# Four experts on three tiles of 128 rows, in column groups, and a gather that skips empty places

## What is computed

```python
def hierarchical_moe(x, ...):
    lg = (xt @ w_router_group + b_router_group)
    gsel = argmax(lg); pgsel = softmax(lg)[gsel]
    le_sel = (xt @ w_router_expert[gsel] + b_router_expert[gsel])
    vals, eidx = lax.top_k(le_sel, 2)
    pw = softmax(vals) * pgsel
    out = sum over the two experts e of pw[e] * (silu(x @ gate[e]) * (x @ up[e])) @ down[e]
y = layer_norm(alpha * h + out)
```

## Time and profile before

| | us |
|---|---|
| median of three runs | 1551.05 (1545.45 to 1553.15) |
| profiled execution, its own time | 1560.32 |
| its span | 1558.7 |
| PE busy in the span | 1439.7 (92%), 5,707 matmul and as many weight load records |
| DVE busy | 724.5 (46%) |
| bytes moved | 221.89 MB |
| granted PE clock, mean | 0.966 |

### The profile page before, as it was taken

The page is one execution under the profiler, slowest core; times in us unless marked ns, Lnnn a source line. Parts: engine busy times, 40 slices in busy tenths (PEclk is TensorE's granted clock), DMA queues, the critical chain, the costliest instruction groups (busy, mean ns, idle before and its releaser), DMA issues. The chain is left out here.

```text
span 1558.7 us, 17701 instructions
## 1 busy us (share of the span) xinstructions
PE 1439.7 (92%) x5707; PEld 782.1 (50%) x5707; DVE 724.5 (46%) x1639; ACT 297.2 (19%) x656; POOL 254.4 (16%) x308
## 2 busy tenths in 40 slices
PE   7999999799999999898989898999489999999985
PEld 2444444344566666565757564555244444444431
DVE  0201023788888889954648444566411111111125
ACT  0100122221221111102554200000011111111114
POOL 3131000133310000201351000011112111121103
PEclk9999999799999999998999899999689999999998
DMA  9221001400122111101331196111089999989835
GB/s 312 69 65 35 15 15 69 129 0 1 41 95 75 70 61 61 70 19 51 92 92 62 55 345 260 28 37 32 15 334 337 347 342 345 352 337 354 325 125 227
DMA packets 72474, 221.89 MB, mean 142 GB/s; under 512 B 16634, under 2 KB 42234, under 8 KB 62042
## 3 DMA queue, kind: packets, MB, share of 16 engines
q1 hardware_dynamic: 56138, 184.64, 33.0%
q0 software_dynamic: 14992, 35.90, 6.6%
q10 hardware_dynamic: 1280, 0.53, 0.2%
HBM read 190.56 MB, written 38.84 MB: 147 GB/s over the span
## 5 line engine op out<-in xcount | busy, mean ns | idle before, releaser
L1786 PE MATMUL main_ps_experts<-w_gate_up,main_e_rowsT 128*128 128x512 f32 x512 | 227.7, 598 | 1.2 <-DVE main_e_rowsT L1891 1.2
L906 DVE TENSOR_SCALAR_CACHE_REDUCE front<-score,bound 128x384 bf16<-128x384 f32 (+2 forms) x198 | 174.2, 943 | 19.2 <-DVE bound L932 18.9
L234 PE MATMUL ps_front<-front,x_all 128*128 128x512 f32 (+1 forms) x448 | 180.4, 557 | 1.7 <-ACT wi L364 1.7
L1786 PEld LDWEIGHTS main_ps_experts<-w_gate_up,main_e_rowsT 128*128 128x128 f32 x512 | 95.7, 192 | 110.6 <-issue 110.6
L234 PEld LDWEIGHTS ps_front<-front,x_all 128*128 128x128 f32 x448 | 83.2, 190 | 91.7 <-issue 81.2
L1896 DVE TENSOR_TENSOR main_hidden<-main_hidden,main_ps_experts 128x256 f32<-128x256 f32 x32 | 13.5, 421 | 221.1 <-ACT main_hidden L1843 221.1
L1520 PE MATMUL ps_merge<-w_o,mergedT 128*128 128x512 f32 x256 | 113.4, 601 | 3.0 <-DVE h_rows L1651 3.0
L733 PE MATMUL ps_gate<-x_all,w_gate 128*128 128x344 f32 x384 | 116.0, 461 | 0.0
L1813 PE MATMUL main_ps_experts<-w_down,main_hiddenT 128*128 128x512 f32 x256 | 115.3, 593 | 0.5 <-ACT main_hiddenT L1848 0.5
L733 PE MATMUL ps_gate<-x_all,front 128*128 128x344 f32 x384 | 113.2, 453 | 0.0
L733 PEld LDWEIGHTS ps_gate<-x_all,w_gate 128*128 128x128 f32 x384 | 74.3, 194 | 38.9 <-issue 2.4
(11 more groups left out here) (296 smaller groups left out, 1784.0 us busy)
## 6 DMA issues: line engine op xcount, KB each, us to landing
w_gate_up<-in_w_gate_up SPq DMA_DIRECT2D x32, 2048.0 KB, 8.7
w_down<-in_w_down SPq DMA_DIRECT2D x32, 1024.0 KB, 11.9
w_gate_up<-pair_out SPq DMA_DIRECT2D x8, 1024.0 KB, 12.0
front<-in_w_qkvi SPq DMA_DIRECT2D x8, 930.0 KB, 20.0
w_gate<-in_w_gate SPq DMA_DIRECT2D x4, 1280.0 KB, 6.0
front<-in_w_gate SPq DMA_DIRECT2D x4, 1280.0 KB, 5.9
h_rows<-in_x_rows SPq DMA_DIRECT2D x9, 512.0 KB, 6.0
h<-h_rows SPq DMA_DIRECT2D x18, 256.0 KB
```

Of the source, the lines that this page charges most:

```text
L234: mm = nc.tensor.matmul(ps[:, g % 2, 0:c1 - c0], x_all[:, k, t * P:(t + 1) * P], w[:, k, c0:c1], start=(k == 0), stop=(k == KC - 1))
L906: V.tensor_scalar(waste[0:n, at - width:at], s, column(bound, g), None, compare, ALU.add, accum_out=column(number, g)).then_inc(taken, 1)
L1786: mm = nc.tensor.matmul(ps[:, GU, :], rowsT[j][:, k, :], w_gu[jw][:, k, :], start=(k == 0), stop=(k == KC - 1))
```

## The change

Lists are cut into shares of 96 ranks. The shares of four experts fill three tiles of 128 rows ("packs"), 24 in all where there were 32 tiles: expert 0 takes rows 0 to 95 of the first, expert 1 its rows 96 to 127 and rows 0 to 63 of the second, expert 2 the other half of that and rows 0 to 31 of the third, expert 3 the rest. A list longer than 96 would bring a second pass. The matmuls of a pack go by column groups, four of 32 or two of 64, each with its own expert's weights as the moving operand. Gate/up and down weights get semaphores of their own, and a buffer is refilled as soon as its own last reader is through. The loop is unrolled. `place` works out lane, tile and share. The gather gets a bound, so that places past a list's end are skipped; the first two gathers still fetch 128 rows (their numbers are clamped), so that the buffers hold finite numbers.

```diff
+SHARE = 96
+QUAD = 4
+PACKS = N_EXPERTS // QUAD * 3
+PARTS = (((0, 32, 0), (32, 64, 0), (64, 96, 0), (96, 128, 1)), ((0, 64, 1), (64, 128, 2)),
+         ((0, 32, 2), (32, 64, 3), (64, 96, 3), (96, 128, 3)))
...
-                step(V.scalar_tensor_tensor(marked, ps[:, 3 + i % 2, 0:N_EXPERTS], float(N_EXPERTS), expert[:],
-                                            ALU.mult, ALU.add))
+                ranks = ps[:, 3 + i % 2, 0:N_EXPERTS]
+                step(V.tensor_scalar(share, ranks, 683.0, None, ALU.mult))
+                step(V.tensor_scalar(share, share, 16, None, ALU.logical_shift_right))
...
+                step(V.scalar_tensor_tensor(marked, wrap, 1.0 - P * PACKS, address, ALU.mult, ALU.add))
                 for which in range(2):
-                    step(V.tensor_tensor(waste, choice[which][i % 2][:], marked, ALU.mult))
-                    step(V.tensor_reduce(slot[:, which:which + 1], waste, AX.X, ALU.add))
+                    step(V.scalar_tensor_tensor(waste, choice[which][i % 2], 1.0, marked, ALU.mult, ALU.mult,
+                                                accum_out=slot[:, which:which + 1]))
...
-                if j >= 2:
-
-                    sp.wait_ge(rows_in[j - 2], 16)
-                load(j, j)
+            for e in range(loaded, W_BUFS):
+                load_gate_up(e)
+                load_down(e)
...
-                    sp.wait_ge(down, (i * W_BUFS + (j - W_BUFS)) * 2 + 2)
-                    load(i * W_BUFS + j, j)
+            for g in range(1, N_EXPERTS // QUAD):
+                e, s = g * QUAD, 3 * (g - 1)
+                sp.wait_ge(gate_up, s + 1)
+                load_gate_up(e)
+                sp.wait_ge(gate_up, s + 2)
+                load_gate_up(e + 1)
+                sp.wait_ge(down, 2 * s + 2)
+                load_down(e)
+                sp.wait_ge(gate_up, s + 3)
+                load_gate_up(e + 2)
+                load_gate_up(e + 3)
+                sp.wait_ge(down, 2 * s + 4)
+                load_down(e + 1)
+                sp.wait_ge(down, 2 * s + 6)
+                load_down(e + 2)
+                load_down(e + 3)
...
-                                            in_offset=bass.IndirectOffsetOnAxis(ap=tokens[:, e:e + 1], axis=0)
-                                            ).then_inc(rows_in[e % 2], 16)
+                                            in_offset=bass.IndirectOffsetOnAxis(ap=tokens[:, e:e + 1], axis=0),
+                                            bounds_check=TOK - 1, oob_is_err=False).then_inc(rows_in[e % 2], 16)
...
-                    mm = nc.tensor.matmul(ps[:, GU, :], rowsT[j][:, k, :], w_gu[jw][:, k, :], start=(k == 0), stop=(k == KC - 1))
+                    for c0, c1, b in PARTS[s % 3]:
+                        mm = nc.tensor.matmul(ps[c0:c1, GU, :], rowsT[j][:, k, c0:c1], w_gu[b][:, k, :],
+                                              start=(k == 0), stop=(k == KC - 1))
...
-            staggered(pe, N_EXPERTS, [(2, turn_hidden), (1, make_hidden), (0, turn_rows), (2, make_result)], W_BUFS)
+            staggered(pe, PACKS, [(2, turn_hidden), (1, make_hidden), (0, turn_rows), (2, make_result)], 2, loop=False)
...
-        with nc.If(longest > P):
+        with nc.If(longest > SHARE):
```

More of the change, by code:

```diff
@@ L1380, in merge_and_route @@
         empty = h[:, TILES - 1, 0:SLOTS // P].bitcast(U32)
-        fall, expert = sb("fall", [P, N_EXPERTS]), sb("expert", [P, N_EXPERTS])
+        fall, lane, column = (sb(n, [P, N_EXPERTS]) for n in ("fall", "lane", "column"))
         valid, away = sb("valid", [P, TILES]), sb("away", [P, TILES])
@@ L1389, in merge_and_route @@
         lgT = over[0:ROUTER, D + 3 * N_EXPERTS:D + 3 * N_EXPERTS + P]
-        choice = [[sb(f"choice{n}_{j}", [P, N_EXPERTS]) for j in range(2)] for n in range(2)]
-        both = [sb(f"both{j}", [P, N_EXPERTS]) for j in range(2)]
+        FREE = D + 3 * N_EXPERTS + P
+        free = [over[:, FREE + n * N_EXPERTS:FREE + (n + 1) * N_EXPERTS] for n in range(10)]
+        choice = [free[2 * n:2 * n + 2] for n in range(2)]
+        both = free[4:6]
+        share, lin, address, wrap = free[6].bitcast(I32), free[7], free[8], free[9]
         slot = sb("slot", [P, 2])
@@ L1688, in sem @@
             return nc.alloc_semaphore(f"{tag}_{name}")
-        ident, tokens, entries, w_gu, w_dn = (keep[n] for n in ("ident", "tokens", "entries", "w_gate_up", "w_down"))
-        w_in = keep["w_in"] if loaded else [sem(f"w_in{j}") for j in range(W_BUFS)]
+        ident, w_gu, w_dn = (keep[n] for n in ("ident", "w_gate_up", "w_down"))
+        tokens, entries = (keep[n][:, 0:PACKS] for n in ("tokens", "entries"))
+        w_gu_in, w_dn_in = (keep[n] if loaded else [sem(f"{n}{j}") for j in range(W_BUFS)] for n in ("w_gu_in", "w_dn_in"))
         rows = [sb(f"e_rows{j}", [P, D]) for j in range(2)]
@@ L1723, in _, with load_gate_up, load_down @@
         def _(sp):
[L1724 to L1730, removed]
-                if j >= 2:
-                    sp.wait_ge(rows_in[j - 2], 16)
-                load(j, j)
+            def load_gate_up(e):
+                sp.dma_start(w_gu[e % W_BUFS][:], ins["w_gate_up"][e]).then_inc(w_gu_in[e % W_BUFS], 16)
+            def load_down(e):
+                sp.dma_start(w_dn[e % W_BUFS][:], ins["w_down"][e]).then_inc(w_dn_in[e % W_BUFS], 16)
+            lists = scratch["list_of"].rearrange("(c p n) o -> c p (n o)", p=P, n=PACKS)
+            sp.dma_start(entries, lists[bass.ds(chunk, 1)]).then_inc(list_in, 16)
+            for e in range(loaded, W_BUFS):
+                load_gate_up(e)
+                load_down(e)
             if loaded:
@@ L1740, in _ @@
                                  ).then_inc(keep["f_const_in"], 16)
[L1741 to L1745 removed]
+            for g in range(1, N_EXPERTS // QUAD):
[14 more added lines that the diff above has]
+                load_down(e + 3)
             if loaded:
[L1747 removed]
+                sp.wait_ge(down, 2 * PACKS)
                 for j in range(2):
[L1749 removed]
+                    sp.wait_ge(stored[j], 16 * PACKS // 2)
                 last.sync(sp)
@@ L1754, in _ @@
             pool.wait_ge(tokens_ready, 1)
-            for e in range(N_EXPERTS + 3):
-                if e < N_EXPERTS:
+            for e in range(PACKS + 3):
+                if e < PACKS:
                     if e >= 2:
@@ L1903, in read_down @@
                 nc.vector.tensor_copy(result[j][:, 512:D], ps[:, 5 + 2 * j, :]).then_inc(down_dve, 1)
[L1905 removed]
+            staggered(dve, PACKS, [(1, multiply), (0, read_rows), (2, read_down)], 2, loop=False)
             if loaded:
@@ L2162, in build @@
         keep["w_down"] = [sb(f"w_down{j}", [P, F // P, D], side="right") for j in range(W_AHEAD)]
-        keep["w_in"] = [whole.enter_context(nc.semaphore(f"w_in_expert{j}")) for j in range(W_BUFS)]
+        keep["w_gu_in"], keep["w_dn_in"] = ([whole.enter_context(nc.semaphore(f"{n}_expert{j}")) for j in range(W_BUFS)]
+                                            for n in ("w_gu_in", "w_dn_in"))
         for name, shape, dt in (("router_logits", [P, TILES, ROUTER], F32), ("weights", [P, 2, TILES], F32),
```

64 lines of the change are left out of this document (38 added, 26 removed).

## The result

The change takes 1476.14 us (median of 4 runs, 1475.54 to 1480.27); the kernel before, on the same chip, 1550.64. The ratio is 0.9543, 95% interval 0.9511 to 0.9574, or 71 us of 1551. The profiled execution took 1475.57, with a span of 1474.1.

What follows compares the result with a forecast made beforehand. PE was taken to bound the experts stage before, the loads after. Last result at 1433.3 + 3.7 for routing = 1437.0 instead of 1503.8, 66.8 us less: 1551.05 - 66.8 = 1484 us, range 1466 to 1520.

Steps and rivals of the forecast that it cites:

- PE's own end: Experts stage: last result at 1420.0 us if PE alone set the pace, with 23 packs of 11.35 after the first product.
- A pack costs what an expert cost, 11.35: Experts stage: column groups overlap, so a pack takes 11.35 us and 24 stand where 32 stood.
- So I charge nothing: PE in the experts stage: turning between full width and column groups was taken to cost nothing, 0.13 us at most.
- The loads set the pace at 395 GB/s: Experts stage: transfers at 395 GB/s put the last result at 1433.3 us, later than PE's 1420.0.
- The later start: Start of the experts stage: first gather lands later among weight loads, first product ends at about 1151.2 us, +6.
- Routing +3.7: Routing: `place` has 12 DVE instructions instead of 6, lengthening routing by 3.7 us (between 2 and 5).
- Finish is the same: Finish, behind the experts stage: its 55 us hardly touched by the change.
- the lower rate: Rival, experts stage: full queues don't hold 395 GB/s; 1510 us at 359, 1526 at 340; chance 0.14.
- the fallen clock: Rival, experts stage: PE's clock falls in its waits, five waits losing 3 us each, 1499 us; chance 0.04.
- fetched rows: Rival, gathers: skipped rows are fetched all the same, 3.9 MB more, 10 us, 1494 us; chance 0.04.
- instruction supply: Rival, unrolled experts stage: PE waits for its instruction blocks, up to 1644 us; chance 0.05.
- Groups in series: Rival, packed matmuls: column groups don't overlap in a long row, +492 us, 2040 us; chance 0.03.

Runs made afterwards that it cites:

- e9: The kernel before with only the gathers' skip of places past a list's end, still 32 tiles; ratio 1.0005 to the kernel before.
- e3: The change with full-width matmuls and half of each weight block loaded from expert 4 on; stage 292.2 us, ratio 0.9452 to the kernel before.
- e11: The change with steps grouped by width, groups of 32, POOL's scatter a step later, first weight loads behind two gathers; stage 299.0 us, ratio 0.9502.
- e1: The change with full-width matmuls using one expert's weights instead of column groups, all loads kept; stage 298.1 us, ratio 0.9511 to the kernel before.
- e12: The change with the first tile of each three in groups of 96 and 32 columns; stage 410.4 us, ratio 1.0192 to the kernel before.
- e7: The change with PE, ACT and DVE steps put together by width and all groups of 32; stage 343.6 us, 1511.1 us.

## Why the prediction was right

The time was forecast at 1484, it was 1476.1, and the range held it. The sum was 66.8 us less; the ratio gives 71. The largest step, a quarter of PE's work in the stage, carried the direction and most of the size. That the number came so close is luck: PE's own end was forecast 11.6 us too early (1420.0 for 1431.6) and the loads' 15.4 too late (1433.3 for 1417.9), as worked out below, and the wrong one of the two was taken as the bound.

- *What bounds before*: PE's products. e9 takes 7.9 MB of transfers away from it and the time stays.
- *A pack costs what an expert cost, 11.35*: the matmuls do (7.07 against 7.03, 3.65 against 3.60), the pack doesn't. **"So I charge nothing" is the step that failed.** Four changes of width cost 0.15 us each, 0.6 a pack and 14 over the stage. e3, without changes and without the loads' limit, takes 13.6 less, and packs with two changes last 11.68. (The Trainium skill, "TensorEngine Tiling (Array Packing)", Key Properties, says that a change of mode drains the array; I held against it. The runs agree with the page: the weight loads no longer run ahead across a change.) The earlier trace rows held the loss, but I misread them. The merged rows show one shape; kept apart, a quarter of the full-width records move only 324 columns and not 512 (17 to 43 us: line, shapes, count | us busy, mean ns of one | idle before):

```profile
L219 PE MATMUL ps_front<-front,x_all 128*128 128x512 f32 x36 | 18.0, 610 | 0.0
L219 PE MATMUL ps_front<-front,x_all 128*128 128x324 f32 x12 | 4.2, 436 | 0.0
```

At 6.87 / 16 = 0.43 us for a record of 512 and 0.27 for one of 324, six and two of them and the small set's two would take 3.98 us, and the period is 4.31. By this estimate a change there and back costs some 0.33, about twice 0.15, and not the 0.13 at most that I took.
- *The loads set the pace at 395 GB/s*: they didn't. They ran at 410 and could do 418 to 420. By the prediction's own formula, 420 for 395 puts the end of the last result at 1417.9 in its time scale (1126.2 + 1.5 + 9 + 102.4 / 0.420 + 37.4), while PE's own end, with packs of 11.98, lies at 1125.8 + 305.8 = 1431.6 on the same scale. What I forecast as the loads' 307.5 us from request to end was PE's 305.8. (The Trainium skill, "DMA: Bandwidth & Descriptors", Specifications, has some 358 GB/s of HBM per core; 410 over 205 us on this one core are more.)
- *The later start*: the first product was to end 25.4 us after the request (1151.2 - 1125.8); it ended 24.7 after it (1140.05 - 1115.36).
- *Routing +3.7*: +3.6 between the same marks, but that it is so close is luck too. The same routing code took 240.2 (e11) to 244.7 us (e1) in other executions, and the old one 238.6 in e9. `place` itself grew from 1.28 to 2.39, so by 1.1 and not 1.6 us; the rest I didn't take apart.
- *Finish is the same*: it was 54.9 and 55.0 us with the old routing and lists (before, e9) and 52.0 to 53.4 in all other runs. Why it is 2 us shorter is open.
- *Rivals*: the lower rate, the fallen clock (1.00 from 1150 to 1400 us), fetched rows and instruction supply didn't come about. Groups in series did not either, and e12 shows that the rival was worth naming.
- *Signs*: PE waiting for weights at every third pack, about 3 us, was wrong for the change. In e1, where PE is quicker, it came from the middle of the stage on, with steps 0.6 to 2.2 us longer. The queues were full from 1180 on as forecast, at 410 and not 390 to 400 GB/s, and the first gather landed 8.9 us after its issue (10 forecast).

## What to carry to other kernels

Where a matmul's columns are partly empty, packing several small problems in equal column groups of 32 or 64 gives the whole array back, but each switch between full width and groups cost 0.15 us here, so steps of one width should stand together. Before reordering an engine's steps, follow the queue that refills its inputs: in e7, with its gathers behind scatters, the stage was 38 us longer where the reorder was to make it 5 to 7 shorter. Before reading a price out of a merged row, look at the shapes in it. When two resources are near their limits, halve one of them in an experiment before believing either.

## What the runs showed of the hardware

- A DMA share of 1.00 was not the limit: 410 GB/s read 1.00, and 418 and 420 read 1.01 in the same stretch with more asked for.
- A weight load did not go ahead of the running matmul across a change between 128 and 32 or 64 columns; within one kind it did. The change cost 0.14 to 0.16 us.
- Groups of 96 and 32 columns ran one after the other, at 1.0 us a pair, 0.15 more than two full ones one after the other (0.85).
- A gather that skips rows has as many packets and fewer bytes.
- Attention, the same code in all runs, took 149 to 151 us in nine profiled executions and 162 to 163 in five; only in the five did PE wait there for DVE's copies (4.8 to 8.6 us). With this and what routing varied, the experts stage began between 1109 and 1135 us, a spread larger than what any experiment after the change gained.
